# Hybrid attention: probabilities times V by token, sums and norms for eight heads at once, outputs turned back, output slabs in token halves

## What is computed

```python
def mla_attention(q_nope, q_rope, k_nope, k_rope, v):      # 8 heads of 64
    s = (q_nope @ k_nope.T + q_rope @ k_rope.T) * 96 ** -0.5, causal
    return softmax(s) @ v
def dilated_attention(q, k, v):                            # 8 heads of 64
    ...                                                    # three dilations, merged by their softmax sums
def hybrid_mixer(h, ...):
    z = h @ w_in                                           # latents, k_rope, and q, k, v of the dilated heads
    ...
    o_mla = mla_attention(q_nope, q_rope, k_nope, k_rope, v_mla)
    o_dil = dilated_attention(qd, kd, vd)
    merged = concatenate([rmsnorm_2(o_mla, grp_gain[:512]), rmsnorm_2(o_dil, grp_gain[512:])])
    return merged @ w_out                                  # 1024 x 1024
```

## Time and profile before

| | us |
|---|---|
| median of 3 executions | 1841.08 |
| lowest, highest | 1835.86, 1845.5 |
| the profiled execution | 1842.03 |
| its span | 1840.4 |
| PE busy | 1734.6 (94%) |
| DVE busy | 1216.6 (66%) |
| ACT busy | 896.8 (49%) |
| mean granted clock of PE | 0.973 |

### The profile page before, as it was taken

The page is one execution under the profiler, slowest core; times in us unless marked ns, Lnnn a source line. Parts: engine busy times, 40 slices in busy tenths (PEclk is TensorE's granted clock), DMA queues, the critical chain, the costliest instruction groups (busy, mean ns, idle before and its releaser), DMA issues.

```text
span 1840.4 us, 29946 instructions
## 1 busy us (share of the span) xinstructions
PE 1734.6 (94%) x11826; PEld 1595.6 (87%) x11826; DVE 1216.6 (66%) x1599; ACT 896.8 (49%) x1235; POOL 122.2 (7%) x163
## 2 busy tenths in 40 slices
PE   6987899999899999999998999988999999999996
PEld 4986799989799998999896899978999896799986
DVE  7889787777765546555676665556655676765556
ACT  4572433356544335434476544345433557644345
POOL 2023111111010000000011000000000003000000
PEclk9998899999999999999999999998999999999999
DMA  9775598868345453555340555434555532355551
GB/s 380 280 292 182 209 358 315 308 232 312 144 172 206 182 183 134 199 193 189 136 178 10 184 200 187 177 138 148 196 193 182 172 138 69 126 184 185 180 197 42
DMA packets 61924, 353.79 MB, mean 192 GB/s; under 512 B 6522, under 2 KB 9738, under 8 KB 27792
## 3 DMA queue, kind: packets, MB, share of 16 engines
q1 hardware_dynamic: 40064, 281.24, 42.2%
q0 software_dynamic: 18384, 66.66, 10.1%
q10 hardware_dynamic: 3392, 4.72, 0.8%
HBM read 349.45 MB, written 3.15 MB: 192 GB/s over the span
## 4 chain that ended last, share of the span: by engine, by line
PE 78%; DVE 11%; ACT 4%; issue 3%; DMA 3%; POOL 0%; DVEq 0%; ACTq 0%; POOLq 0%
PE bank L528 23%; PE bank L529 23%; PE bank L530 23%; DVE w_lo L1509 2%; ACT w_hi L1021 2%; PE bank L560 1%; PE bank L562 1%; PE bank L561 1%; DMA shared<-in_mods 1%; PE bank L700 1%; DVE shared L1530 1%; PE bank L721 1%; DVE shared L2046 1%; PE bank L710 1%; DVE x L2055 1%
## 5 line engine op out<-in xcount | busy, mean ns | idle before, releaser
L528 PE MATMUL bank<-a_hi,w_hi 128*128 128x256 f32 x2648 | 758.8, 287 | 11.0 <-DVE a_lo L1577 3.6
L529 PE MATMUL bank<-a_lo,w_hi 128*128 128x256 f32 x2648 | 754.6, 285 | 0.0
L530 PE MATMUL bank<-a_hi,w_lo 128*128 128x256 f32 x2648 | 754.5, 285 | 0.0
L528 PEld LDWEIGHTS bank<-a_hi,w_hi 128*128 128x128 f32 x2648 | 513.9, 194 | 17.8 <-issue 11.5
L529 PEld LDWEIGHTS bank<-a_lo,w_hi 128*128 128x128 f32 x2648 | 514.0, 194 | 2.9 <-issue 0.7
L530 PEld LDWEIGHTS bank<-a_hi,w_lo 128*128 128x128 f32 x2648 | 513.5, 194 | 0.0
L1771 DVE TENSOR_TENSOR w_lo<-raw,w_hi 128x2048 fp32r<-128x2048 f32 x144 | 330.0, 2292 | 258.2 <-ACT w_hi L1162 258.2
L1162 ACT CAST w_hi<-raw 128x2048 fp32r<-128x2048 f32 x144 | 273.9, 1903 | 268.9 <-PE bank L530 268.9
L1509 DVE TENSOR_TENSOR w_lo<-raw,w_hi 128x2048 fp32r<-128x2048 f32 x119 | 272.1, 2292 | 133.5 <-ACT w_hi L1021 133.4
L1021 ACT CAST w_hi<-raw 128x2048 fp32r<-128x2048 f32 x122 | 231.3, 1907 | 90.9 <-PE bank L530 84.4
L528 PE MATMUL bank<-w_hi,hid_hi 128*128 128x512 f32 x548 | 215.8, 394 | 4.8 <-DVE hid_lo L2192 3.0
(11 more groups left out here) (242 smaller groups left out, 1948.8 us busy)
## 6 DMA issues: line engine op xcount, KB each, us to landing
raw<-in_stream SPq DMA_DIRECT2D x266, 1024.0 KB, 4.8
shared<-in_mods POOLq DMA_DIRECT2D x102, 512.0 KB, 6.3
grow<-in_rows POOLq DMA_DIRECT2D x12, 512.0 KB, 4.0
work<-in_mods POOLq DMA_DIRECT2D x8, 512.0 KB, 9.7
bias_rows<-work ACTq DMA_DIRECT2D x1, 2048.0 KB, 19.0
x<-in_x_t SPq DMA_DIRECT2D x1, 1024.0 KB, 6.2
x<-in_x_d ACTq DMA_DIRECT2D x1, 1024.0 KB, 4.9
work<-bias_rows ACTq DMA_DIRECT2D x1, 1024.0 KB, 10.5
```

Source lines behind the costliest of these rows:

```text
L528: pe.matmul(out, w_h, v_h, start=start, stop=False, skip_group_check=True)
L529: pe.matmul(out, w_h, v_l, start=False, stop=False, skip_group_check=True)
L530: return pe.matmul(out, w_l, v_h, start=False, stop=stop, skip_group_check=True)
```

## The change

All of it is in the two mixers of the second block (`by_token`); the attention of the first block is as it was.

- PE multiplies by token: the turned probabilities (128 keys x 128 queries) are the stationary operand, V's 64 columns stream, and each head adds 64 columns to a bank of 128 tokens x 512 features. Banks 4 and 5 hold the dilated heads, 6 and 7 the MLA heads. The probabilities are not normalised.
- ACT's exponentials keep their sums for all heads (`esum`). DVE takes one reciprocal for eight heads and multiplies the banks with it (`outputs`), at step 9 for the dilated heads, after the heads for the MLA ones, and squares the dilated outputs by token at step 11; ACT squares the MLA ones.
- The group norm is a number per token: `outputs_rsqrt` on ACT (step 14 for the dilated heads), `outputs_normed` on DVE, which scales the outputs in place.
- PE turns the scaled outputs back to features (`turn_outputs`, step 15 for the dilated heads), ACT and DVE make `a_hi` and `a_lo` from the bank with the group gain (`outputs_hi`, `outputs_lo`). The four `norm_stat` of the two layers go.
- The out slabs: pieces of token half 0 of slabs 0 and 1, then the MLA outputs are turned, then token half 1 of slabs 0 and 1, then slabs 2 and 3.
- Out slab 1 is split at step -1 (ACT) and step 0 (DVE) of the attention instead of after it.

```diff
-L_QLAT, L_KVLAT, L_GDIL, L_GMLA = range(4)
-NORM_CHUNKS = [CH] + [2, 1, 4, 4] * LAYERS2
+L_QLAT, L_KVLAT = range(2)
+NORM_CHUNKS = [CH] + [2, 1] * LAYERS2
...
+        esum = sb("esum", [P, 2, 2, HEADS])
+        erec = sb("erec", [P, 2, 2, HEADS])
...
-                    pe.wait_ge(pn_done, heads[k] + 1)
+                    if by_token:
+                        pe.wait_ge(exp_done, heads[k] + 1)
+                    else:
+                        pe.wait_ge(pn_done, heads[k] + 1)
...
+                    if by_token:
+                        pt, (value, out) = prob_t[:, heads[k] % 2], pv(k)
+                        pe.matmul(out(0), pt[:, 0:P], value(0), start=(k % HEADS == 0), stop=True, skip_group_check=True)
+                        pe.matmul(out(1), pt[:, P:2 * P], value(0), start=(k % HEADS == 0), stop=False, skip_group_check=True)
+                        pe.matmul(out(1), pt[:, 2 * P:3 * P], value(1), start=False, stop=True, skip_group_check=True).then_inc(pv_done, 1)
+                        return
...
+                    return lambda kt: v[:, kt, h * 64:(h + 1) * 64], lambda t: bank[4 + 2 * (k // HEADS) + t][:, h * 64:(h + 1) * 64]
+                def turn_outputs(g):
+                    for t in range(2):
+                        pe.wait_ge(o_scaled, 4 * l + 2 * g + t + 1)
+                        for c in range(4):
+                            mm = pe.transpose(bank[(4, 0)[g] + c // 2][:, (c % 2) * S + t * P:(c % 2) * S + (t + 1) * P],
+                                              f_tok[:, t, group_at(g) + c * P:group_at(g) + (c + 1) * P], ident[:, :])
+                            if t == 1 and c % 2:
+                                mm.then_inc(o_turned, 1)
...
-                          {-1: queries, 0: copied, HEADS - 3: mla_ready, NORM_STEP: lambda: norm_stat(norm2(l, L_GDIL)),
-                           16: lambda: out_slab(0, (2, 3))})
-                pe.wait_ge(o_done, 8 + 8 * l + 7)
+                          {-1: queries, 0: copied, HEADS - 3: mla_ready, 15: lambda: turn_outputs(0)}, True)
                 out_slab(0, (0,))
-                pe.wait_ge(o_done, 8 + 8 * l + 8)
-                out_slab(0, (1,)).then_inc(slab_done, 1)
-                norm_stat(norm2(l, L_GMLA))
-                for i in range(1, 4):
+                pe.wait_ge(nl_ready, before(APPLY_CHUNKS, apply2(l, LA_GDIL)) + 4)
+                out_slab(0, (1,))
+                out_slab(1, (0, 1))
+                turn_outputs(1)
+                out_slab(0, (2, 3)).then_inc(slab_done, 1)
+                out_slab(1, (2, 3)).then_inc(slab_done, 1)
+                for i in (2, 3):
...
+                        total = esum[:, k // HEADS, t, k % HEADS:k % HEADS + 1] if by_token else ssum[:, h % 2, t:t + 1]
                         ins = act.activation(dst[:, h % 2, lo:hi], src[:, h % 2, lo:hi], ACT.Exp, scale=-1.0,
-                                             bias=nmax[:, h % 2, t:t + 1], accum_out=ssum[:, h % 2, t:t + 1])
+                                             bias=nmax[:, h % 2, t:t + 1], accum_out=total)
...
-                steps = {0: queries, NORM_STEP + 1: lambda: rsqrt(norm2(l, L_GDIL), 512)}
-                steps.update({min(2 * c + 4, NORM_STEP - 1): lambda c=c: dilated_square(c) for c in range(4)})
-                steps.update({NORM_STEP + 3 + c: lambda c=c: dilated_hi(c) for c in range(4)})
-                attention([HEADS + 16 * l + k for k in range(16)], None, steps)
-                warm_up()
-                squares(norm2(l, L_GMLA), lambda c: f[:, c, :], lambda c: act.wait_ge(o_done, o0 + 5 + c))
+                def outputs_rsqrt(g):
+                    act.wait_ge(o_squared, 4 * l + 2 * g + 2)
+                    act.activation(out_rs, out_sums, ACT.Abs_reciprocal_sqrt, scale=1.0 / 512, bias=eps[:, :]).then_inc(o_rs_ready, 1)
+                def outputs_hi(g):
+                    for b2 in range(2):
+                        act.wait_ge(o_turned, 4 * l + 2 * g + b2 + 1)
+                        for m in range(2):
+                            c = (4, 0)[g] + 2 * b2 + m
+                            act.activation(a_hi[:, c, :], bank[(4, 0)[g] + b2][:, m * S:(m + 1) * S], ACT.Copy,
+                                           scale=col("group2", CH * l + c)).then_inc(nh_ready, 1)
+                attention([HEADS + 16 * l + k for k in range(16)], None,
+                          {-1: lambda: split_to(b + 12), 0: queries, 14: lambda: outputs_rsqrt(0)}, True)
+                outputs_hi(0)
+                for t in range(2):
+                    act.wait_ge(o_tok_ready, 4 * l + 2 + t + 1)
+                    square_into(f_tok[:, t, 0:512], sq[:, 2 * t:2 * t + 2, :].rearrange("p c s -> p (c s)"), out_sums[:, t:t + 1]).then_inc(o_squared, 1)
+                outputs_rsqrt(1)
                 split_to(b + 13)
-                rsqrt(norm2(l, L_GMLA), 512)
-                normed_hi(apply2(l, LA_GMLA), a_out)
+                outputs_hi(1)
...
-                    if 0 <= k + 1 < n:
+                    if 0 <= k + 1 < n and not by_token:
                         normalise(k + 1)
                     if k + 3 < n:
                         scores(k + 3)
-                    if k >= 1:
+                    if k >= 1 and not by_token:
...
+                def outputs(g):
+                    h0 = HEADS + 16 * l + 8 * g + 8
+                    dve.wait_ge(exp_done, h0)
+                    dve.reciprocal(erec[:, g, :, :], esum[:, g, :, :]).then_inc(rs_done, 1)
+                    dve.wait_ge(rs_done, HEADS + 2 * l + g + 1)
+                    dve.wait_ge(pv_done, h0)
+                    for t in range(2):
+                        dve.tensor_tensor(f_tok[:, t, group_at(g):group_at(g) + 512].rearrange("p (h e) -> p h e", h=HEADS),
+                                          bank[4 + 2 * g + t][:, :].rearrange("p (h e) -> p h e", h=HEADS),
+                                          erec[:, g, t, :].unsqueeze(2).to_broadcast([P, HEADS, 64]), ALU.mult).then_inc(o_tok_ready, 1)
+                def dilated_squares():
+                    for t in range(2):
+                        v = f_tok[:, t, 512:1024]
+                        dve.wait_ge(o_tok_ready, 4 * l + t + 1)
+                        dve.tensor_tensor_reduce(sq[:, 4 + 2 * t:6 + 2 * t, :].rearrange("p c s -> p (c s)"), v, v, 1.0, 0.0,
+                                                 ALU.mult, ALU.add, out_sums[:, t:t + 1]).then_inc(o_squared, 1)
+                def outputs_normed(g):
+                    dve.wait_ge(o_squared, 4 * l + 2 * g + 2)
+                    n = 3 * (2 * l + g)
+                    dve.tensor_scalar(out_mean, out_sums, 1.0 / 512, EPS, ALU.mult, ALU.add).then_inc(o_step, 1)
+                    dve.wait_ge(o_rs_ready, 2 * l + g + 1)
+                    dve.scalar_tensor_tensor(out=out_a, in0=out_rs, scalar=-0.5, in1=out_rs, op0=ALU.mult, op1=ALU.mult).then_inc(o_step, 1)
+                    dve.wait_ge(o_step, n + 2)
+                    dve.tensor_tensor(out_b, out_a, out_mean, ALU.mult).then_inc(o_step, 1)
+                    dve.wait_ge(o_step, n + 3)
+                    dve.scalar_tensor_tensor(out=out_r, in0=out_b, scalar=1.5, in1=out_rs, op0=ALU.add, op1=ALU.mult).then_inc(o_r_ready, 1)
+                    dve.wait_ge(o_r_ready, 2 * l + g + 1)
+                    for t in range(2):
+                        v = f_tok[:, t, group_at(g):group_at(g) + 512]
+                        dve.wait_ge(o_tok_ready, 4 * l + 2 * g + t + 1)
+                        dve.tensor_scalar(v, v, out_r[:, t:t + 1], None, ALU.mult).then_inc(o_scaled, 1)
+                def outputs_lo(g):
+                    at = before(APPLY_CHUNKS, apply2(l, (LA_GDIL, LA_GMLA)[g]))
+                    for i in range(4):
+                        c = (4, 0)[g] + i
+                        dve.wait_ge(nh_ready, at + (i | 1) + 1)
+                        dve.scalar_tensor_tensor(out=a_lo[:, c, :], in0=bank[(4, 0)[g] + i // 2][:, (i % 2) * S:(i % 2 + 1) * S],
+                                                 scalar=col("group2", CH * l + c), in1=a_hi[:, c, :].bitcast(F32),
+                                                 op0=ALU.mult, op1=ALU.subtract).then_inc(nl_ready, 1)
+                attention([HEADS + 16 * l + k for k in range(16)], lambda k: mask[:, 1 if k < HEADS else 0, :], None,
+                          {-1: lambda: split_to(b + 11), 0: lambda: split_to(b + 12), 1: queries, 9: lambda: outputs(0), 11: dilated_squares}, True)
+                outputs_normed(0)
+                outputs_lo(0)
+                outputs(1)
+                outputs_normed(1)
                 split_to(b + 13)
-                root(norm2(l, L_GMLA), 512)
-                normed(apply2(l, LA_GMLA), norm2(l, L_GMLA), lambda c: f[:, c, :], lambda c: col("group2", CH * l + c), a_h, a_l)
+                outputs_lo(1)
```

(5 more changed lines are left out.)

48 lines of the change are left out of this document (10 added, 38 removed).

## The result

The changed kernel takes **1828.71 us** (median of 11 runs, 1827.4 to 1832.53), the kernel before, run beside it on the same chip, 1839.82 (11 runs, 1835.85 to 1845.5). The ratio is **0.9943**, 95% interval 0.9932 to 0.9954: faster by 0.57%. On the 1841.08 that the prediction started from, that ratio is 1830.6. Forecast were 1836.0, with 0.73 on "within 0.5%" and 0.22 on "faster".

What follows compares the result with a forecast made beforehand. PE was taken to bound the kernel, at 1.97 us a steady head. The terms left 2.6 us won a layer, 5.2 in all, taking the profiled 1842.03 to 1836.8, forecast as 1836 us; range 1829 to 1843.

Steps and rivals of the forecast that it cites:

- V by token: V's product on PE: six 128-wide passes replace the old two matmuls, 0.79 us either way, no gain or loss per head.
- the seam: Extra 0.15 us in V's product on PE, put down to a matmul group that begins behind a wait.
- Neither bound: Limits for V's product: streaming alone gains 0.32 us a head, load and streaming in turn loses 0.32; 3.5 us a layer.
- narrow passes are cheap: Rival for V's product: passes cost only their streaming, 7 us more gain, 1829.8 us; chance 0.14.
- The rule of the Trainium skill: Rival for V's product: weight loads don't overlap matmuls in the same row groups, 7 us less gain, 1843.9 us; chance 0.03.
- Normalising leaves VectorE: Attention heads: no gain in steady heads; the third head's 1.77 us wait goes, but the first transposes start later.
- The first layer's sum: First layer, from first transposes at 967.08 to the out slabs' end at 1023.8 instead of 1026.47: 2.6 us won.
- The 56.7 us given as the mark: Sign of being right: time from a layer's first transposes to the end of its out slabs, where before had 61.3.
- The rotated queries: POOL's work behind DVE's query products: ends at 975.9, PE asks at 976.0, so 0.1 us of cover.
- I count this as chance: Second layer's attention before the change: some 10.2 us at half clock, costing 3.26 us, taken as chance.
- half clock in both layers: Sign of being wrong: PE's granted clock at half level in the changed stages of both layers.
- The rival of the falling clock: Half clock at four new PE idle places, before first transposes and turn_outputs(0), 3.4 us each: 1850 us; chance 0.07.

Runs made afterwards that it cites:

- e1_wide_v: The kernel before, with V's product taking the 128 columns of a head pair as weights instead of 64; 1835.34 us, 0.9984 of the kernel before.
- e2_old_v: The changed kernel with V's product back in its old form, two matmuls a head with 64-wide weights; 1835.08 us, 0.9974 of the kernel before.
- e7_norm_back: The changed kernel with DVE's normalising of every head put back and PE waiting for it; 1838.89 us, 1.0002 of the kernel before.
- e6_warm_start: The changed kernel with twelve small warming products on PE in the wait before each layer's first transposes; 1828.0 us, 0.9939 of the kernel before.
- e3: The changed kernel with out slab 1 split behind the heads on ACT and DVE; 1827.45 us, 0.9949 of the kernel before.
- e9: The changed kernel with out slab 1 split at step 6 of the heads on ACT and DVE; 1825.1 us, 0.9935 of the kernel before.
- e10: e9 plus warming products on PE, four before the query copies' wait and eleven before the outputs' first turn; 1825.38 us, 0.993 of the kernel before.
- e8: The changed kernel with the MLA outputs turned after 12 out-slab products instead of 24; 1830.33 us, 0.9959 of the kernel before.
- e5: The kernel before, with V's product always written to rows 0 to 63 of the bank; 1837.63 us, 0.9992 of the kernel before.
- e4: The changed kernel with PE's turn_outputs(0) at step 16 and ACT's root of the dilated outputs at 15; 1830.34 us, 0.9948 of the kernel before.

## Why the prediction was right or wrong

**V by token: the step that failed.** The prediction had the right pace for the narrow passes and the wrong owner for the seam: "A group that begins behind a wait also has a seam", "0.64 + 0.15 = 0.79: I take no gain and no loss per head". The passes go at 0.112 us (979.78 to 980.01 are two), near to the 0.106 of the earlier trace rows. But the 0.15 does not belong to a group that begins behind a wait. It belongs to the change between 64-wide and 128-wide weights, and the groups beside V paid it too: in e1_wide_v, where only the width changed, the transposes lose 0.09, V 0.14 and the scores 0.10, together 0.33. After has 0.09, 0.18 and 0.05, together 0.32, so six narrow passes add nothing to that. Neither bound had this reason. The gain per head is as large as that of the rival "narrow passes are cheap", whose mechanism did not come; the range reached down to 1829 only for this rival, so that it holds 1830.6 is luck. The trace of before had the answer: in the first block's attention, where V's weights are 128 wide, PE's timeline reads
```profile
461.56 0.49 PE L710 MATMUL bank<-ident,work 128*128 128x128 f32 x3
461.89 0.60 PE L721 MATMUL bank<-work 128*128 128x256 f32 x2
462.32 0.38 PE L722 MATMUL bank<-work 128*128 128x128 f32 x2
462.54 0.82 PE L700 MATMUL bank<-work 128*128 128x128 f32 x4
```
0.33 and 0.65 where the earlier trace rows have 0.42 and 0.79, from the same lines of the kernel. The nearest rows for a new shape were those of the same group with the wider weights, in the same kernel, and I had gone to a norm's sums.

The rule of the Trainium skill that I weighed against the change ("TensorE: Matmul & The Clock Gate", "The mechanism": loads overlap running matmuls only in another row group) had the smallest chance, and after bears against it. All its weights fill the same 128 rows, yet from 976 to 988, where PE is busy all the time, the weight loads (PEld) are busy for 11.30 of the 12.00 us; and a pass of 64 columns takes 0.112 us where one of 128 takes 0.11 (three transposes in 0.33), though by load and stream in turn they would be 0.053 apart. The same section also has loads into a background weight buffer pulled ahead of running matmuls, which I left out; whether these loads are such, no run here shows.

**Normalising leaves VectorE.** "In the steady heads PE hides them: nothing" holds for a head of 1.97 us (e2_old_v: 0.9974, as forecast). It was not carried on to the rivals. With heads of 1.64 to 1.66 us it depends on what else VectorE has: with the copies of head pairs it is late in every second head (e1_wide_v: 1.90), without them it keeps up in the steady heads and is late beside every one-off piece of work (e7_norm_back: 4.8 and 3.5 us a layer). So the term is nothing or nearly everything, by the other one.

**The first layer's sum, term by term.** First transposes 967.04, forecast 967.08: right. Fourth head 974.32 for 972.06: +2.3, of which the half clock is 2.9 (7.28 us from the first transposes, 4.36 in e6_warm_start) and the seams -0.6. From there to head 12: 14.90 for 17.73, -2.8, the seams. From head 12 to the turned outputs 6.3 for 6.7, with PE held 2.60 for 2.4. From these to out slab 0 3.74 for 3.8. Out slabs 22.8 for 23.5: the second turn takes 0.79 for 1.0, and the seams of 0.5 that I had added are hardly there. Together 1022.05 for 1023.8: that is so near because the half clock's 2.9 hides most of the 3.4 that the seams give, and this too is luck. MLA's scaling ended at 1004.0 and was asked for at 1004.83, 0.8 us of cover for the 0.7 forecast; VectorE's row in after:
```profile
1003.11 0.89 DVE L2220 TENSOR_SCALAR shared<-shared,stat 128x512 f32<-128x512 f32 x2
```
The 56.7 us given as the mark were 55.0 and, in the second layer, 55.8.

**The rotated queries.** Forecast with 0.1 us of cover. POOL ended at 976.5 instead of 975.9, and after waited for nothing only because the half clock had made PE late. With shorter heads and full clock PE asks much earlier than the forecast 976.0, in e6_warm_start at 974.8: in all layers with short heads and without half clock there (e3, e6, e9, e10, the second of e8) it waited 0.74 to 0.76 us. So by the sixth head the first layer's half clock has cost 2.1 us and not 2.9 (977.63 against 975.56).

**The clock.** "I count this as chance" was too little. What I had named as a sign of error, half clock in both layers, is in the profile: both layers have it at the 2.83 us wait for the query copies (from 966.3, while PE waits, and from 1529.5, behind the wait), and one behind the turned outputs. The rival of the falling clock was half right: three of its four new places show half clock (6.8, 3.4 and 6.8 us), and the one that can be priced cost 2.9 us up to the fourth head, near the 3.4 that I had put for one. Its 1850 did not come, since the seams gave more, and since before had 10.2 us of half clock of its own around the second layer. With the split moved and both waits filled it is gone from the stages (e10_split_mid_warm; with the split moved alone, e9_split_mid keeps 6.8 and 3.4 us), and the medians hardly follow. From 898 us on and outside the stages, after has another 40.1 us at half clock and e10_split_mid_warm 42.7; what decides of those stays open. The other executions say the same of the clock: its mean was 0.975 in before (53 executions beside e1 to e8), 0.971 in after (11) and 0.974 in e9 and e10 (6 each). In the 29 executions of before beside e5 to e8, 0.001 less of mean clock went with 1.1 us more, so after's lower clock would be worth some 4 us, an estimate; of these the medians of e9 and e10 show 1.5 and 2.4.

## What to carry to other kernels

Read the pace of a matmul group in its neighbours: where groups with weights of different width alternate, price the seam of each change, and look in the same trace for the same group with equal widths before you go to another kind of row. When an engine that paces a loop gets faster, work out the next engine's period at once: here the wider weights alone gave 0.16%, all the rest without them 0.26%, and both together 0.57% (that this is more than the sum, the intervals don't show; the waits for VectorE do show that the two depend on each other). A stage that profiles 5 us shorter may show only half of it in the medians; compare ratios before a refinement is believed.

## What the runs showed of the hardware

- Alternating 128-wide and 64-wide fp32 weights cost 0.33 us per head over three groups (0.42, 0.79, 0.76 in before against 0.33, 0.65, 0.66 in e1_wide_v; after has 0.33, 0.61, 0.71), whichever 64 output rows are written (e5_same_rows). I had not expected that the groups before and behind the narrow one pay as well.
- Six fp32 passes with 128-wide weights and 64 columns took 0.61 us; a pass took 0.112 within the group (979.78 to 980.01 are two), as with 128 columns (three transposes 0.33). Half the columns in all (384 instead of 768) took 0.04 us off V (0.65 in e1_wide_v), and the scores behind it were 0.05 longer.
- Where PE waited 2.8 us for the query copies, the granted clock was 0.50 within the first heads in 8 of 10 cases (after, e2, e4, e7, e8, two layers each; not in the second layer of e2 and e8). Where the wait was 1.0 us or filled with 4 or 12 warming products, it was 1.00 up to the third head's transposes in all 14 (before, e1, e3, e5, e6, e9, e10).
